# Gated DeltaNet mixing loop: the in-chunk couplings made, masked and turned four heads at a time, the cross-chunk couplings behind them

## The chip, the cores and the metric

The kernel runs on one core of one Trainium2 chip. The metric is the device time of one launch in microseconds. Before the change the median of three runs is 1443.28 us (lowest 1442.0, highest 1451.61).

## What is computed

One inference step of a one-layer decoder trunk: RMSNorm, one input projection, two head groups side by side (sliding-window attention and a gated DeltaNet), an output projection, a mixture of experts, a per-layer embedding and a last norm. There are 1024 prompt tokens and 8 decode tokens, all float32. The part that the change touches is the DeltaNet in its chunked form. For each head and each chunk of 64 tokens the reference makes

```python
A = jnp.where(strict, jnp.einsum('bhncd,bhnjd->bhncj', kb, k) * decay, 0.0)
sol = lax.linalg.triangular_solve(eye + A, rhs, left_side=True, lower=True, unit_diagonal=True)
u, w = sol[..., :dv], sol[..., dv:]
qk = jnp.where(causal, jnp.einsum('bhncd,bhnjd->bhncj', q, k) * decay, 0.0)
...
v_new = u_c - jnp.einsum('bhcd,bhde->bhce', w_c, S)
o = jnp.einsum('bhcd,bhde->bhce', qg_c, S) + jnp.einsum('bhcj,bhje->bhce', qk_c, v_new)
S = S * gl_c[..., None, None] + jnp.einsum('bhcd,bhce->bhde', kd_c, v_new)
```

so each 64x64 matrix `eye + A` (8 heads, 16 chunks) has to be inverted or solved with, before the state `S` can go from one chunk to the next.

## The kernel before

The kernel runs stage by stage, each engine with a program of its own and semaphores between them. The mixing stage walks over 8 tiles of 128 prompt tokens: tile 0 stands by itself (it also carries the decode tokens' output projection), tiles 1 to 7 are a loop. A tile holds two chunks of 64 tokens, one on the lower 64 partitions and one on the upper 64 (`HB[0]` and `HB[1]`), and all eight heads along the free dimension. A group `g` is four heads; `hs` is its slice.

The inverse of `eye + A` is built by doubling. `MT` begins as the unit matrix. Level 0 copies the couplings that its mask allows from `ATd` into `MT`; then each of five levels turns `MT` into `T_` on VectorE, multiplies `ATd` by `T_` on TensorE into PSUM, copies that to `Xs` on ScalarE, multiplies `Xs` by `MT` on TensorE, and copies what the level's mask allows into `MT` on VectorE again. The VectorE half is `fill(t, l)` (masked copy at line 1163, turn at line 1166, both four heads at a time and 128x256). The TensorE half is `level(t, l)`: for both groups the first product, which waits for that group's `T{g}`, then for both groups the second, which waits for that group's `X{g}` (all at line 1431, 16 small matmuls for each group and product, 64 for a level). In level 1 the second products also wait for `S`, the state update of line 1089.

What stands around it, in the order in which each engine's program is written:

- VectorE (`tile`): norms and decays of this tile; the outputs of the tile before (line 1104 ends that, `gated`); the small rows at lines 1200 to 1204; then the couplings. Line 1209 multiplies the Gram matrix `G` (PSUM) by the decays `E_` into `ATd`, all eight heads, once for each chunk (64x512, two instructions); line 1212 waits for both and multiplies `ATd` by `betn` in place (128x512); line 1213 makes `ATo`, the couplings of the second chunk to the first (64x512); line 1214 calls `fill(t, 0)`. Then `state` (line 1089), `gated_out` (lines 1108 to 1113), `largest(t, 1)` (lines 1139 to 1144) and `fill(t, 1)`.
- TensorE (`tile`): the Gram matrices (line 1482), the state increments (1393), twelve output-projection matmuls of the tile before (line 1405, 128x512), `level(t, 1)`, then the query-key products (line 1492), which wait for `ATo` because they write the PSUM banks that it reads, `level(t, 2)`, `turn_out` (1399), `level(t, 3)`, and on.
- ScalarE: the exponentials of `E_`, those of attention group 0, then the two copies of level 1 (line 1322), those of attention group 1 (they wait for `largest(t, 1)`, line 1144), then the copies of level 2.
- GpSimd: the mask of the decays (`Em`, line 1042, 128x1024) and then two powers of 128x8 (line 1025), about when VectorE makes the couplings.

A VectorE instruction that reads what the one before it wrote waits on a semaphore that this one raises; there are such waits before line 1212 (`ATd`) and between the masked copy and the turn (`MT{g}`). No queue of DMAs is issued from the touched lines.

Of the kernel before, what the change touches and what calls it, by code (L numbers as in the profile page):

```python
# [29 lines left out]
ALU = mybir.AluOpType  # L30
# [10 lines left out]
AH, HD, GQA = 8, 64, 4  # L41
# [89 lines left out]
def bc(ap, n):  # L131

    return ap.unsqueeze(2).to_broadcast([ap.shape[0], ap.shape[1], n])


def bm(ap, n):

    return ap.unsqueeze(1).to_broadcast([ap.shape[0], n, ap.shape[1]])
# [7 lines left out]
def program(nc, I, O):  # L146
# [3 lines left out]
    def S(name):  # L150
        if name not in sems:
            sems[name] = nc.alloc_semaphore(name=f"{name}_{len(stages)}")
        return sems[name]
# [14 lines left out]
    def settle(eng):  # L168

        eng.sem_inc(S(f"settled_{eng.engine}".replace(".", "_")), 1)  # L170
# [4 lines left out]
    with es:  # L175
# [55 lines left out]
        def flat(i, n):  # L231
            return psum[:, i:i + n, :].rearrange("p a b -> p (a b)")
# [715 lines left out]
        E_ = mem.take(NH, P)  # L948
        gU = mem.take(NH, P)
        ATd, ATo = mem.take(NH, HD), mem.take(NH, HD)  # L950
# [9 lines left out]
        ss8, m8, r8, egam, kdec, eglS, gam8, rqp, rq2, bet, betn, rk2, kab = (mem.take(NH) for _ in range(13))  # L960
# [4 lines left out]
        HB = (slice(0, HD), slice(HD, P))  # L965
# [22 lines left out]
        def four(i):  # L988
            return heads(bank(i)[:, 0:4 * HD])

        with nc.Block() as block:
# [71 lines left out]
            def _(v):  # L1063
                V = nc.vector
# [84 lines left out]
                    v.wait_ge(S(f"v_den{g}"), t + 1)  # L1149
                    V.reciprocal(rcp[g], den[g]).then_inc(S(f"rcp{g}"), 1)  # L1150

                def fill(t, l):

                    for g in range(2):
                        hs = slice(4 * g, 4 * g + 4)
                        if l == 0:
                            v.wait_ge(S("ATn"), t + 1)
                            v.wait_ge(S("eye"), t + 1)
                        else:
                            v.wait_ge(S(f"PT{g}_ps"), LV * t + l)  # L1160
                        settle(v)
                        mask = cst[:, C_LV + l * P:C_LV + l * P + HD].bitcast(I32)
                        V.copy_predicated(MT[:, hs], bm(mask, 4), ATd[:, hs] if l == 0 else four(6 + g)).then_inc(S(f"MT{g}"), 1)  # L1163
                        if l < LV:
                            v.wait_ge(S(f"MT{g}"), (LV + 1) * t + l + 1)
                            V.transpose(T_[:, hs].rearrange("p h d -> p (h d)"), MT[:, hs].rearrange("p h d -> p (h d)")).then_inc(S(f"T{g}"), 1)  # L1166

                def tile(t, R, dst, first=False):
# [36 lines left out]
                    v.wait_ge(S("E"), t + 1)  # L1205
                    v.wait_ge(S("G_ps"), t + 1)
                    G = flat(4, 2).rearrange("p (h i) -> p h i", i=P)
                    for b in range(2):
                        V.tensor_tensor(ATd[HB[b]], G[HB[b], :, HB[b]], E_[HB[b], :, HB[b]], ALU.mult).then_inc(S("ATd"), 1)
                    v.wait_ge(S("ATd"), 2 * t + 2)  # L1210
                    v.wait_ge(S("v_betn"), t + 1)
                    V.tensor_tensor(ATd, ATd, bc(betn, HD), ALU.mult).then_inc(S("ATn"), 1)
                    V.tensor_tensor(ATo[HB[0]], G[HB[0], :, HB[1]], E_[HB[0], :, HB[1]], ALU.mult).then_inc(S("ATo"), 1)
                    fill(t, 0)
                    if not first:
                        state(t - 1)
                        gated_out(t - 1)
                    largest(t, 1)
                    fill(t, 1)
                    v.wait_ge(S("QK_ps"), t + 1)  # L1220
                    v.wait_ge(S("Em"), t + 1)
                    V.tensor_tensor(QK, flat(4, 2).rearrange("p (h i) -> p h i", i=P), Em, ALU.mult).then_inc(S("QK"), 1)
                    fill(t, 2)
                    v.wait_ge(S("vraw"), t + 1)
                    v.wait_ge(S("v_kab"), t + 1)
# [18 lines left out]
                v.wait_ge(L("wr"), 32)  # L1244
                V.tensor_tensor(wr, wr, bc(g_ffn, NG + NE), ALU.mult).then_inc(S("wr_gain"), 1)
                tile(0, DEC, lg[0:DEC, NT, :], first=True)
                with v.Fori(1, NT) as t:
                    tile(t, P, lg[:, bass.ds(t - 1, 1), :].rearrange("p a n -> p (a n)"))
# [1051 lines left out]
```

## Time and profile before

| | us |
|---|---|
| median of three runs | 1443.28 |
| the three runs | 1442.0, 1443.28, 1451.61 |
| the profiled execution's own time | 1437.78 |
| its span, from first to last instruction | 1436.0 |
| what lies around the span | 1.78 |
| mean granted TensorE clock over the span | 0.947 |
| TensorE busy (matmul) | 1273.1 |
| VectorE busy | 620.6 |
| ScalarE busy | 375.3 |
| GpSimd busy | 208.6 |

The mixing loop takes from about 380 to 800 us of the span. In the views, PE is TensorE, PEld its weight loads, DVE is VectorE, ACT is ScalarE, POOL is GpSimd. "decode_and_mix" is the room in SBUF that all tiles of this stage share, so the groups have to be told apart by line. A row of a timeline gives start (us from the span's start), length, engine, line, operation, shapes, count, and in brackets the idle time before it with what ended it. A row of the windows gives the stretch, its length, and the busy time (and number of instructions) of PE, PEld, DVE, ACT and POOL, then the granted clock (1.00 is full), the DMA share and GB/s.

### The profile page before, as it was taken

The numbers are of one execution on the slowest core, as the hardware profiler recorded it, in microseconds if no ns is written. First come the engines' busy times: TensorE is split into PE (matmuls) and PEld (weight loads), VectorE is DVE, ScalarE is ACT, GpSimd is POOL, SyncE is SP. The second block draws the span as 40 slices with busy tenths as digits, with TensorE's granted clock in tenths as the row PEclk, the third lists the DMA queues.
The fourth block names the chain that finished last, engine by engine and source line by source line (L and its number), as shares of the span: only waits on it lengthen the run. The fifth ranks groups of instructions, "written<-read, shape, count | busy, mean of one in ns | idle before, by whom it ended". The sixth has DMA issues, their size and how long they took to land. (4 is left out here: it accounts for less than half of the span.)

```text
span 1436.0 us, 21846 instructions
## 1 busy us (share of the span) xinstructions
PE 1273.1 (89%) x8380; PEld 876.8 (61%) x8380; DVE 620.6 (43%) x1130; ACT 375.3 (26%) x735; POOL 208.6 (15%) x275
## 2 busy tenths in 40 slices
PE   6999999954698899999898759899999999974997
PEld 4669999942466676676676534444444454434776
DVE  2323555127756756757757134121111112106564
ACT  2322223111234334334434112111111111113332
POOL 0000000002211212212312001122222222110110
PEclk9999999985899999999999779999999999996999
DMA  6211223237320220220220149499999999935451
GB/s 206 90 52 60 88 88 88 76 43 222 94 66 15 78 91 10 81 91 2 89 77 4 44 153 390 151 350 347 339 341 344 352 353 344 345 144 220 150 175 46
DMA packets 151335, 226.08 MB, mean 157 GB/s; under 512 B 12651, under 2 KB 123835, under 8 KB 146670
## 3 DMA queue, kind: packets, MB, share of 16 engines
q1 hardware_dynamic: 130606, 171.27, 36.1%
q10 hardware_dynamic: 11184, 28.48, 5.6%
q0 software_dynamic: 9504, 25.77, 4.6%
q8 instruction: 27, 0.44, 0.1%
q14 instruction: 14, 0.11, 0.0%
HBM read 183.37 MB, written 46.76 MB: 160 GB/s over the span
## 5 line engine op out<-in xcount | busy, mean ns | idle before, releaser
L1657 PE MATMUL psum<-experts 128*128 128x512 f32 x528 | 232.2, 593 | 2.6 <-DVE experts L1679 2.6
L627 PE MATMUL psum<-split_parts 128*128 128x344 f32 x1224 | 194.2, 321 | 0.0
L627 PEld LDWEIGHTS psum<-split_parts 128*128 128x128 f32 x1224 | 193.9, 188 | 0.1
L1657 PEld LDWEIGHTS psum<-experts 128*128 128x128 f32 x528 | 100.5, 191 | 128.0 <-issue 125.0
L1694 DVE COPY experts<-psum 128x256 f32<-128x256 f32 x33 | 14.0, 425 | 274.8 <-PE psum L1664 274.8
L1431 PE MATMUL psum<-decode_and_mix 64*64 64x64 f32 x2560 | 100.8, 228 | 28.7 <-DVE decode_and_mix L1166 21.3
L1431 PEld LDWEIGHTS psum<-decode_and_mix 64*64 64x64 f32 x2560 | 89.2, 140 | 57.3 <-issue 56.8
L1405 PE MATMUL psum<-decode_and_mix 128*128 128x512 f32 x256 | 120.9, 618 | 0.7 <-ACT decode_and_mix L1288 0.7
L1673 PE MATMUL psum<-experts 128*128 128x512 f32 x264 | 119.2, 595 | 1.5 <-ACTq L1710 1.0
L2260 PE MATMUL psum<-last_parts 128*128 128x512 f32 x432 | 103.1, 399 | 0.0
L2260 PEld LDWEIGHTS psum<-last_parts 128*128 128x128 f32 x432 | 82.9, 194 | 17.1
L1025 POOL TENSOR_TENSOR decode_and_mix<-decode_and_mix,lasting 128x8 f32<-128x8 f32 (+2 forms) x33 | 44.0, 1342 | 314.6 <-DVE decode_and_mix L1123 234.9
L1405 PEld LDWEIGHTS psum<-decode_and_mix 128*128 128x128 f32 x256 | 47.7, 196 | 51.3 <-issue 48.8
L1673 PEld LDWEIGHTS psum<-experts 128*128 128x128 f32 x264 | 47.8, 191 | 49.2 <-issue 47.2
L1641 POOL DMA_INDIRECT ye_d<-experts x33 | 33.2, 1006 | 272.0 <-ACT experts L1708 272.0
L1708 ACT ACTIVATE experts<-psum 128x1024 f32<-128x1024 f32 x33 | 33.8, 1023 | 139.0 <-PE psum L1673 139.0
L1701 ACT ACTIVATE experts<-psum 128x256 f32<-128x256 f32 x33 | 12.6, 383 | 196.9 <-PE psum L1657 196.9
L587 PE MATMUL psum<-project 128*128 128x512 f32 x144 | 63.6, 595 | 0.0
L1322 ACT ACTIVATE decode_and_mix<-psum 128x256 f32<-128x256 f32 x80 | 30.5, 381 | 124.0 <-PE psum L1431 121.6
L1679 DVE TENSOR_TENSOR experts<-psum,lasting 128x1024 f32<-128x1024 f32 x33 | 40.4, 1225 | 47.6 <-PE psum L1649 47.6
L1163 DVE COPY_PREDICATED decode_and_mix<-lasting,psum 128x256 f32<-128x256 int32 x80 | 33.6, 430 | 48.6 <-PE psum L1431 48.6
L422 DVE SCALAR_TENSOR_TENSOR project<-project 128x1056 f32<-128x1056 f32 x36 | 47.5, 1319 | 4.7 <-DVE project L418 1.5
(369 smaller groups left out, 1692.0 us busy)
## 6 DMA issues: line engine op xcount, KB each, us to landing
experts<-in_w_gate SPq DMA_DIRECT2D x33, 1024.0 KB, 5.8
experts<-in_w_up SPq DMA_DIRECT2D x33, 1024.0 KB, 10.6
experts<-in_w_down SPq DMA_DIRECT2D x33, 1024.0 KB, 12.3
project<-in_w_in SPq DMA_DIRECT2D x18, 512.0 KB, 4.9
last<-ye_d SPq DMA_DIRECT2D x16, 512.0 KB, 7.1
conv_out_d<-project ACTq DMA_DIRECT2D x12, 512.0 KB, 3.1
decode_and_mix<-conv_out_d SPq DMA_DIRECT2D x8, 768.0 KB, 7.4
until_mixed<-in_x_prompt SPq DMA_DIRECT2D x8, 512.0 KB
```

The costliest lines, as they stand in the source:

```text
L422: nc.vector.scalar_tensor_tensor(yc[:, u, 0:NV], xp[:, u, j:j + NV], cwT[:, ft, j:j + 1], yc[:, u, 0:NV], ALU.mult, ALU.add).then_inc(S(f" ...
L587: mm = nc.tensor.matmul(bank(5 + 2 * u), xT[:, u, k, :], wtok[:, k, 144:], start=(k == 0), stop=(k == KD - 1))
L627: mm = nc.tensor.matmul(thirds(u)[:, b], w[:, u, k, :], x[:, k, b * TB:(b + 1) * TB], start=(i == 0 and k == 0), stop=(i == 2 and k == KD ...
L1025: g.tensor_tensor(out, in_, half[0:out.shape[0]].to_broadcast([out.shape[0], n]), ALU.pow).then_inc(S("r_" + name), 1)
L1163: V.copy_predicated(MT[:, hs], bm(mask, 4), ATd[:, hs] if l == 0 else four(6 + g)).then_inc(S(f"MT{g}"), 1)
L1405: mm = T.matmul(bank(2 + n)[0:R], src[:, k, :], wout[:, k, n * 512:(n + 1) * 512], start=(k == 0), stop=(k == KD - 1))
L1431: mm = T.matmul(bank(out + g)[HB[b], (s % 4) * HD:(s % 4 + 1) * HD], left[HB[b], s, :], right[HB[b], s, :], start=True, stop=True)
L1657: mm = nc.tensor.matmul(bank(2 + s.v), xgT[s.v][:, k, :], wgu[s.u][:, k, :], start=(k == 0), stop=(k == KD - 1))
L1673: mm = nc.tensor.matmul(bank(6 + n), hT[s.v][:, k, :], wd[s.u][:, k, n * 512:(n + 1) * 512], start=(k == 0), stop=(k == KE - 1))
L1679: nc.vector.tensor_tensor(xgT[s.v], flat(0, 2).rearrange("p (k c) -> p k c", c=P), bc(g_ffn, P), ALU.mult).then_inc(S("xgT" + s.h), 1)
L1708: nc.scalar.activation(ye[s.v], flat(6, 2), ACT.Copy).then_inc(S("ye" + s.h), 1)
L2260: mm = nc.tensor.matmul(bank(4 + 2 * (t % 2) + m), x[t % 2][:, k, :], w[:, k, cols], start=(i == 0 and k == 0), stop=(i == 2 and k == KD - 1))
```

## The change

VectorE's program of a tile makes the in-chunk couplings group by group. For four heads it multiplies `G` by `E_` for either chunk (now 64x256 each), waits for the two, multiplies by `betn` (now 128x256), and at once does that group's level 0 of `fill`: masked copy and turn. Then the same for the other four heads. `ATo`, the couplings between the chunks, stood ahead of `fill(t, 0)` and stands behind it now. The semaphores count accordingly: `ATd` rises four times a tile, not two, and `ATn` two times, not one; `fill` at level 0 waits for its own group's count. TensorE, ScalarE, GpSimd and the DMA queues keep their programs.

```diff
-                def fill(t, l):
-
-                    for g in range(2):
+                def fill(t, l, groups=(0, 1)):
+
+                    for g in groups:
                         hs = slice(4 * g, 4 * g + 4)
                         if l == 0:
-                            v.wait_ge(S("ATn"), t + 1)
+                            v.wait_ge(S("ATn"), 2 * t + g + 1)
                             v.wait_ge(S("eye"), t + 1)
...
                     G = flat(4, 2).rearrange("p (h i) -> p h i", i=P)
-                    for b in range(2):
-                        V.tensor_tensor(ATd[HB[b]], G[HB[b], :, HB[b]], E_[HB[b], :, HB[b]], ALU.mult).then_inc(S("ATd"), 1)
-                    v.wait_ge(S("ATd"), 2 * t + 2)
-                    v.wait_ge(S("v_betn"), t + 1)
-                    V.tensor_tensor(ATd, ATd, bc(betn, HD), ALU.mult).then_inc(S("ATn"), 1)
+                    for g in range(2):
+                        hs = slice(4 * g, 4 * g + 4)
+                        for b in range(2):
+                            V.tensor_tensor(ATd[HB[b], hs], G[HB[b], hs, HB[b]], E_[HB[b], hs, HB[b]], ALU.mult).then_inc(S("ATd"), 1)
+                        v.wait_ge(S("ATd"), 4 * t + 2 * g + 2)
+                        v.wait_ge(S("v_betn"), t + 1)
+                        V.tensor_tensor(ATd[:, hs], ATd[:, hs], bc(betn[:, hs], HD), ALU.mult).then_inc(S("ATn"), 1)
+                        fill(t, 0, (g,))
                     V.tensor_tensor(ATo[HB[0]], G[HB[0], :, HB[1]], E_[HB[0], :, HB[1]], ALU.mult).then_inc(S("ATo"), 1)
-                    fill(t, 0)
                     if not first:
                         state(t - 1)
                         gated_out(t - 1)
```

## Rows read from the trace of the kernel before

**Rows 1.** Windows view, one stretch of 50 us inside the mixing loop.

```profile
500.00:550.00 50.00, 47.31 (x558) 34.08 (x554) 32.83 (x74) 18.86 (x42) 11.48 (x8) 1.00 0.21 66
```

**Rows 2.** Waits view, 380 to 800 us: total us, times, longest.

```profile
PE psum L1431 <- DVE decode_and_mix L1166: 21.3, 17, 2.1
```

**Rows 3.** Timeline of PE, tile from 540 us and start of the next.

```profile
539.41 5.42 PE L1405 MATMUL psum<-decode_and_mix 128*128 128x512 f32 x12
546.21 2.73 PE L1431 MATMUL psum<-decode_and_mix 64*64 64x64 f32 x64 [1.38 <-DVE decode_and_mix L1166]
548.87 1.16 PE L1492 MATMUL psum<-decode_and_mix 64*128 64x128 f32 x16
551.35 3.26 PE L1431 MATMUL psum<-decode_and_mix 64*64 64x64 f32 x64 [1.32 <-DVE decode_and_mix L1166]
...
600.75 2.73 PE L1431 MATMUL psum<-decode_and_mix 64*64 64x64 f32 x64 [1.39 <-DVE decode_and_mix L1166]
```

**Rows 4.** Timeline of DVE, the same tile.

```profile
539.68 2.33 DVE L1104 TENSOR_SCALAR decode_and_mix<-decode_and_mix 128x8 f32<-128x8 f32 x1
...
542.39 1.40 DVE L1209 TENSOR_TENSOR decode_and_mix<-psum,decode_and_mix 64x512 f32<-64x512 f32 x2
543.83 0.69 DVE L1212 TENSOR_TENSOR decode_and_mix<-decode_and_mix 128x512 f32<-128x512 f32 x1
544.55 0.68 DVE L1213 TENSOR_TENSOR decode_and_mix<-psum,decode_and_mix 64x512 f32<-64x512 f32 x1
545.16 0.43 DVE L1163 COPY_PREDICATED decode_and_mix<-lasting,decode_and_mix 128x256 f32<-128x256 int32 x1
545.62 0.45 DVE L1166 STREAM_TRANSPOSE decode_and_mix<-decode_and_mix 128x256 f32<-128x256 f32 x1
...
546.79 0.38 DVE L1089 TENSOR_TENSOR decode_and_mix<-decode_and_mix,psum 128x256 f32<-128x256 f32 x1
547.10 0.15 DVE L1108 TENSOR_TENSOR decode_and_mix<-decode_and_mix 128x8 f32<-128x8 f32 x1
...
550.14 0.16 DVE L1144 TENSOR_TENSOR decode_and_mix<-lasting,decode_and_mix 128x4 f32<-128x4 f32 x1
550.28 0.45 DVE L1163 COPY_PREDICATED decode_and_mix<-lasting,psum 128x256 f32<-128x256 int32 x1
...
553.91 0.44 DVE L1163 COPY_PREDICATED decode_and_mix<-lasting,psum 128x256 f32<-128x256 int32 x1 [0.79 <-PE psum L1431]
```

**Rows 5.** Timeline of ACT, the same tile, level 1's first copy.

```profile
546.93 0.38 ACT L1322 ACTIVATE decode_and_mix<-psum 128x256 f32<-128x256 f32 x1 [4.75 <-PE psum L1431]
```

**Rows 6.** Lines by form, DVE, 380 to 800 us: busy, mean ns, idle.

```profile
L1212 DVE TENSOR_TENSOR decode_and_mix<-decode_and_mix 128x512 f32<-128x512 f32 x8 | 5.5, 693 | 0.3
L1239 DVE TENSOR_TENSOR decode_and_mix<-decode_and_mix 128x256 f32<-128x256 f32 x8 | 3.3, 418 | 0.0
```

**Rows 7.** Timelines of PE and DVE, tile 0.

```profile
386.86 2.53 PE L1431 MATMUL psum<-decode_and_mix 64*64 64x64 f32 x64 [2.06 <-DVE decode_and_mix L1166]
390.41 2.40 PE L1431 MATMUL psum<-decode_and_mix 64*64 64x64 f32 x64
388.90 0.45 DVE L1163 COPY_PREDICATED decode_and_mix<-lasting,psum 128x256 f32<-128x256 int32 x1
```

**Rows 8.** Windows view: level 2 of the tile of Rows 3, and of a later tile.

```profile
550.88:555.08 4.20, 3.53 (x67) 3.23 (x68) 3.35 (x7) 2.27 (x10) 0.00 (x0) 0.79 0.00 0
714.47:718.67 4.20, 3.36 (x76) 2.90 (x77) 3.47 (x8) 2.64 (x11) 0.00 (x0) 1.00 0.00 0
```

**Rows 9.** Timeline of PE, level 1 of that later tile and of the next.

```profile
709.83 2.73 PE L1431 MATMUL psum<-decode_and_mix 64*64 64x64 f32 x64 [1.38 <-DVE decode_and_mix L1166]
763.44 2.73 PE L1431 MATMUL psum<-decode_and_mix 64*64 64x64 f32 x64 [1.39 <-DVE decode_and_mix L1166]
```

**Rows 10.** Timeline of POOL, the tile of Rows 3.

```profile
539.63 2.36 POOL L1042 TENSOR_TENSOR decode_and_mix<-decode_and_mix,lasting 128x1024 f32<-128x1024 f32 x1
542.10 3.23 POOL L1025 TENSOR_TENSOR decode_and_mix<-decode_and_mix,lasting 128x8 f32<-128x8 f32 x2
```

## The prediction

> **What bounds the kernel now.** I looked first at the windows view over the mixing loop. In a stretch of 50 us TensorE is busy 47.31 us and VectorE 32.83 [rows 1], so on average TensorE bounds the loop. That is an average; what is left over has to be read from the places where TensorE stands still. The waits view names one place that matters here: the small matmuls of the inverse (L1431) wait for VectorE's turns (L1166), 21.3 us in all, 17 times [rows 2]. That total is the most that this change could ever earn.
>
> The PE timeline shows where in a tile these waits lie. In the tile from 540 us TensorE ends its twelve projection matmuls at 539.41 + 5.42 = 544.83 and stands 1.38 us before level 1 starts at 546.21. Level 1 and the query-key products end at 548.87 + 1.16 = 550.03, and TensorE stands again, 1.32 us, before level 2 at 551.35 [rows 3]. One pair of waits comes in each of the seven looped tiles. The change aims at the first of the pair. Whether it earns anything depends on the second.
>
> So the third view is VectorE's timeline between the two. From 539.68, where L1104 starts, no idle time stands ahead of any VectorE instruction until level 2's masked copy at 553.91, which shows 0.79 us [rows 4]. Between level 0's `fill` and level 1's `fill` stand the state update (546.79), the gated outputs (from 547.10) and the second group's maxima (last one at 550.14). The masked copy of level 1 starts at 550.28, directly behind them. What it reads, the second products of level 1, is nearly done by then: TensorE has gone over to the query-key products at 548.87, so both groups are there 1.4 us before VectorE is. Thus level 2 does not wait for level 1. It waits for VectorE to work through its list. The reader should see two different things in two waits of one name: before level 1, TensorE waits for the couplings; before level 2, it waits for whatever VectorE's list still holds, however early level 1 was done.
>
> **The change, part by part.** It removes nothing and adds three VectorE instructions per tile: four products of 64x256 in place of two of 64x512, two of 128x256 in place of one of 128x512. It moves `ATo` behind level 0.
>
> *The list up to level 1's fill.* Before, from the first coupling (542.39) to the state update (546.79) is 4.40 us [rows 4]. By starts: the two 64x512 products 1.44 (to 543.83), `betn` 0.72 (to 544.55), `ATo` 0.61 (to 545.16), both groups' masked copies and turns 1.63 (to 546.79). The same rows show what a neighbour costs: `betn` lasts 0.69 and the next starts 0.03 after its end, while `ATo` lasts 0.68 and the next starts 0.07 before its end. `betn` follows a wait on its own engine's result; in the new order a wait of that kind also stands behind each `betn`, since the masked copy reads it. So I count length + 0.03 where the next instruction waits for this one, and length - 0.07 where it does not.
>
> The lengths of the halves: the form of the new `betn` is there, 128x256 from SBUF at 418 ns, against 693 ns for the whole 128x512 [rows 6]. For a 64x256 product with one operand in PSUM the nearest rows are that 0.42 and the 0.38 of the 128x256 state update, also with a PSUM operand [rows 4]. I take 0.41, since the whole ones (0.68 to 0.70) are almost as long as `betn`. Per group: first product 0.41 - 0.07 = 0.34, second 0.41 + 0.03 = 0.44, `betn` 0.42 + 0.03 = 0.45, together 1.23. Two groups 2.46, against 1.44 + 0.72 = 2.16 before. The copies, turns and `ATo` keep 1.63 and 0.61. The list grows by 0.30 us. Bounds: with 0.38 for all three forms, 2 x (0.31 + 0.41 + 0.41) - 2.16 = +0.10; with 0.42 for all, 2 x (0.35 + 0.45 + 0.45) - 2.16 = +0.34. A shorter list is excluded, because no work goes away and the rows show that half the elements cost well over half the time. The Trainium skill, VectorE: DVE Perf Modes, section on the TRN2 errata, says that operations from SBUF pay a fixed cost per instruction, about 150 cycles as measured, and advises 512 elements or more; it speaks against the split. At 0.96 GHz (the same page) three extra ones would be an estimated 0.47 us per tile, 3.3 us in seven, where the rows give 0.30 and 2.1.
>
> *The gain ahead of level 1.* The first group's turn now ends about 542.39 + 1.23 + 0.46 + 0.45 = 544.53 (copy to turn 0.46, turn 0.45 long [rows 4]), before TensorE is free at 544.83. The 1.38 us go away, but only for 16 of the 64 matmuls. The second group's turn, which ended about 0.07 behind the state update's start, at 546.86, now ends at about 546.86 - 0.61 + 0.30 = 546.55, so TensorE stops again after about 0.7 us of work. Behind the second group's first product stands the wait for the state update, which the moved `ATo` pushes: it ended at 547.17 and now ends at 547.47. Before, ScalarE's copy of the first group ended at 546.93 + 0.38 = 547.31 [rows 5] and set the second products; now the state update does. So level 1 ends at about the same time as before, 0.1 to 0.2 us earlier. `ATo` itself, needed by the query-key products, is there at 547.2, well before the 548.87 at which they started. That move costs nothing, and if its cover were gone, it would cost its 0.61 us at most.
>
> *Where the stall goes.* Level 1's `fill` starts 0.30 us later, since it is behind VectorE's list; so does the turn that releases level 2, and level 2 starts at 551.65. The stall of 1.38 us is not saved: it is moved behind the first 16 matmuls and then into the wait before level 2. Behind level 2 there is no cover: VectorE waits for TensorE again at 553.91 [rows 4], so 0.30 us per tile goes straight to the end. ScalarE's second exponentials also start behind VectorE's last maximum and shift along.
>
> *Tile 0.* There is no state update and no gated output, and level 2 follows without idle time ahead of it, after 2.06 us ahead of level 1 [rows 7]. Level 1 gains some tenths here, but VectorE's copy at 388.90 also moves by 0.30, which takes them back. I count 0; the bounds are -2.06 and +0.34.
>
> *The clock.* In level 2 of the tile from 540 us the granted clock is 0.79 over the window, in that of a later tile 1.00 [rows 8]: part of the window ran at 1.2 GHz, after the two stops. From level 1 to level 1 the first tile takes 600.75 - 546.21 = 54.54 us and the later one 763.44 - 709.83 = 53.61 [rows 3, 9]: a dip costs 0.93 us. The same two windows laid over all seven looped tiles give four with a dip (0.77 to 0.81) and three at 1.00. The change shifts idle time from before level 1 to before level 2, which could bring a dip to the other three (+2.8 us) or, with other timing, take four away (-3.7 us). I count no change and keep both ends.
>
> *Sum.* 7 x 0.30 = 2.1 us. Against the profiled execution: 1437.78 (span 1436.0 and 1.78 around it) + 2.1 = 1439.9. The median lies 5.5 us above that execution, so on its scale: 1443.28 + 2.1 = **1445.4 us**.
>
> **The rivals.**
>
> *TensorE sets the pace after all.* If VectorE's list had slack that the timeline hides, the 1.38 us would be earned in each looped tile: 7 x 1.38 = 9.7, and 2.06 in tile 0, so 11.7 us: 1443.28 - 11.7 = 1431.6. For it: 21.3 us of waits, and it is the first group's turn that releases level 1. Against it: the unbroken VectorE row and the second wait in the same tile. Even then the gain is 0.8%. Faster by over 1% needs 14.4 us, that is, the second wait must shrink too. I give this 6 in 100 within 1%, and 3 in 100 beyond it together with fewer dips.
>
> *VectorE is held by GpSimd.* L1104, eight elements wide, lasts 2.33 us beside GpSimd's mask product (539.63 to 541.99) and ends with it [rows 4, 10]. Directly behind run GpSimd's two powers, 542.10 to 545.33 [rows 10]. The first group's `betn` and its masked copy now fall inside that stretch (`betn` at 542.39 + 0.34 + 0.44 = 543.17), where the copy used to start at 545.16. If the powers held them as the mask held L1104, `betn` would start at 545.33: 2.16 us per tile, 7 x 2.16 = 15.1 us, so 1445.4 + 15.1 = 1460.5, slower by 1.2%. It decides from 12.3 us on, 1.76 per tile. Against it: before, `betn` itself started at 543.83, within the powers, and lasted the usual 0.69. The Trainium skill, SBUF — State Buffer, section SBUF: two separate sides, says that a VectorE operation in a two-port mode, or with two SBUF inputs, and a GpSimd operation that reads SBUF exclude each other for the whole instruction. L1104 looks like it, and `betn` beside the powers does not. I give it 5 in 100.
>
> *The clock falls in all seven tiles.* 1445.4 + 2.8 = 1448.2, still within 1%. For it: the stop ahead of level 2 grows from 1.32 to about 1.7 us. 20 in 100; dips gone altogether (1441.7), 10 in 100.
>
> **How the numbers follow.** Forecast, VectorE's list sets level 2 and the clock stays as it is: 56. Clock in all seven: 20; in none: 10; TensorE sets the pace: 6, and 3 beyond 1%; GpSimd holds VectorE: 5. About 1% is what a measurement of this kernel can tell from no change, as its three runs are 9.6 us apart. So faster 0.03, same 0.92, slower 0.05. The range takes in the clock's two ends with the list's bounds, 1445.4 - 3.7 - 1.4 = 1440.3 and 1445.4 + 2.8 + 0.3 = 1448.5, and the spread of runs around their median, mostly upward: 1437 to 1452.
>
> **What would show it.** Right, if in the changed trace the idle time ahead of level 1 is near 0, that within level 1 has grown, that ahead of level 2 has grown to 1.5 us or more, and VectorE has no idle time from L1104 to level 1's last turn, with some 4.7 us from the first coupling to the state update. Wrong, if the masked copy of level 1 waits for TensorE (then the gain is real), if a half product or a copy beside GpSimd's powers lasts over 1 us (then it is held), or if the windows of level 2 show a clock other than a mixture of 0.8 and 1.0.

## The result and the profile after

The changed kernel takes 1459.12 us (median of 4 runs, 1454.9 to 1464.11) against 1442.64 us: a ratio of 1.0106 with a 95% interval of 1.0055 to 1.0157. The same kernel timed again beside the experiments gave 1456.6 us (9 runs, 1451.73 to 1459.47) against 1445.94, a ratio of 1.0076 (1.0047 to 1.0105). It is slower by about 1%. The forecast was 1445.4 with a range from 1437 to 1452: the direction of the step was right, its size was not.

The kernel before spreads over 20 us: 85 runs beside the experiments lie between 1435.75 and 1455.58, with a median of 1445.3. Its profiled execution (1437.78) is thus one of its shorter ones. The profiled execution after takes 1456.79 us (span 1455.0, mean granted clock 0.934).

First VectorE's timeline, in the changed kernel, of the tile that answers to [rows 4]:

```profile
553.12 0.87 DVE L1211 TENSOR_TENSOR decode_and_mix<-psum,decode_and_mix 64x256 f32<-64x256 f32 x2
554.02 0.43 DVE L1214 TENSOR_TENSOR decode_and_mix<-decode_and_mix 128x256 f32<-128x256 f32 x1
554.63 0.45 DVE L1163 COPY_PREDICATED decode_and_mix<-lasting,decode_and_mix 128x256 f32<-128x256 int32 x1 [0.18 <-DVE decode_and_mix L1214]
555.11 0.45 DVE L1166 STREAM_TRANSPOSE decode_and_mix<-decode_and_mix 128x256 f32<-128x256 f32 x1
555.59 0.88 DVE L1211 TENSOR_TENSOR decode_and_mix<-psum,decode_and_mix 64x256 f32<-64x256 f32 x2
...
558.06 0.68 DVE L1216 TENSOR_TENSOR decode_and_mix<-psum,decode_and_mix 64x512 f32<-64x512 f32 x1
558.67 0.40 DVE L1089 TENSOR_TENSOR decode_and_mix<-decode_and_mix,psum 128x256 f32<-128x256 f32 x1
...
562.18 0.44 DVE L1163 COPY_PREDICATED decode_and_mix<-lasting,psum 128x256 f32<-128x256 int32 x1
```

From the first coupling to the state update is now 558.67 - 553.12 = 5.55 us, where it was 4.40. The forecast had 4.70. The list is 1.15 us longer, and the rows say by what: a pair of half products takes 0.90 us up to `betn`, so 1.80 for all four where the two whole ones took 1.44; each masked copy of level 0 has an idle time of 0.18 us ahead of it that ends with VectorE's own `betn` product; and behind each turn the next product starts 0.48 us after the turn's start, where it was 0.37 between turn and state update.

Then TensorE's timeline, for the same tile of the changed kernel, the answer to [rows 3]:

```profile
550.13 5.42 PE L1407 MATMUL psum<-decode_and_mix 128*128 128x512 f32 x12
555.70 0.68 PE L1433 MATMUL psum<-decode_and_mix 64*64 64x64 f32 x16
558.17 0.68 PE L1433 MATMUL psum<-decode_and_mix 64*64 64x64 f32 x16 [1.79 <-DVE decode_and_mix L1166]
559.22 1.15 PE L1433 MATMUL psum<-decode_and_mix 64*64 64x64 f32 x32 [0.36 <-DVE decode_and_mix L1089]
560.29 1.16 PE L1494 MATMUL psum<-decode_and_mix 64*128 64x128 f32 x16
563.25 3.64 PE L1433 MATMUL psum<-decode_and_mix 64*64 64x64 f32 x64 [1.79 <-DVE decode_and_mix L1166]
```

Level 1 starts 0.15 us after the projection matmuls (before: 1.38), as the change intends. It then does 16 matmuls and stops for 1.79 us until the second group is turned, stops again for 0.36 until the state update that the moved `ATo` pushed back, and stops for 1.79 ahead of level 2, where it was 1.32. Three stops in place of two, and level 2 starts 563.25 - 553.12 = 10.13 us after the first coupling, where it was 8.96: 1.17 us later, which is the growth of the list.

How long the looped tiles became shows between these two tiles of the changed kernel (first products of level 1). The clock falls to 1.2 GHz for 3.4 us in every looped tile of this execution (such a short fall is called a dip here), but in this one within level 1 and the query-key products, where no time is lost by it, as shown further down:

```profile
611.07 0.68 PE L1433 MATMUL psum<-decode_and_mix 64*64 64x64 f32 x16 [0.15 <-DVE decode_and_mix L1166]
...
665.85 0.68 PE L1433 MATMUL psum<-decode_and_mix 64*64 64x64 f32 x16 [0.15 <-DVE decode_and_mix L1166]
```

54.78 us, against 53.61 for a tile without a dip before [rows 9]: 1.17 us more. In seven looped tiles that is 8.2 us. Where the kernel before has a costly dip, its tile takes 54.54 us [rows 3, 9], and there the changed kernel is only 0.24 us longer: the longer list takes the place of the dip's cost.

Most of the rest is at the end of the loop's first pass. TensorE's timeline there and the window behind it, in the changed kernel:

```profile
469.77 0.64 PE L1420 MATMUL psum<-decode_and_mix 128*128 128x36 f32 x4
471.82 2.57 PE L1420 MATMUL psum<-decode_and_mix 128*128 128x36 f32 x12 [1.41 <-issue]
474.32 1.97 PE L1369 MATMUL psum<-decode_and_mix 64*64 64x64 f32 x16
...
471.50:489.00 17.50, 17.18 (x89) 12.93 (x89) 7.98 (x17) 0.00 (x0) 0.61 (x1) 0.51 0.19 58
```

TensorE waits 1.41 us, in the middle of the routing matmuls, for nothing that these views show, and for 17.5 us from there the granted clock is 0.51, that is 1.2 GHz, while the engine is busy 98% of the time. The 16 small matmuls of line 1369 take 1.97 us in it; a pass later they take 1.14. The first looped tile is 64.2 us long instead of 55.6. Windows of half a microsecond from 380 us to a little behind the loop add up to 30.7 us at 1.2 GHz before and 64.8 after.

The trace's record of transfers tells more of that wait: a 16 KB transfer on a queue named "instruction" runs from 469.32 to 470.46 us, and TensorE goes on 1.36 us after its end. Nine profiles of this study have the wait, and in each TensorE goes on 1.2 to 1.5 us after the end of such a transfer, which began between 466.9 and 473.3 us; in the four without the wait it began between 464.3 and 465.8. So the wait goes with instructions that come late. What makes them late is not shown.

Over the mixing loop, from the first looped tile's couplings to the last state update, the profiled executions differ by 398.53 - 382.50 = 16.0 us: 8.2 of VectorE's list, and 7.8 net of clock and first pass (the first looped tile alone is 8.6 longer, list included). Another 3.0 us lie behind the loop, where VectorE's couplings have no part.

### The profile page after: what moved, and what is told of

Read it like the earlier page. It is cut to its first block and busy times, and to the rows that moved or that the text cites. A ratio compares the mean times of both kernels' runs of the same rounds, so it can differ in the third digit from the quotient of the medians.

```text
span 1455.0 us, 21899 instructions
## 1 busy us (share of the span) xinstructions
PE 1289.3 (89%) x8380; PEld 889.0 (61%) x8380; DVE 626.3 (43%) x1154; ACT 375.4 (26%) x735; POOL 209.0 (14%) x275
```

## The experiments

Each kernel was timed against the kernel before on the same chip; the last section has a single run. The time at 1.2 GHz of a run is worked out as twice (1 - granted clock) times its span, and given as the mean over a kernel's runs. "List" is the time from the first coupling to the state update, and "tile" a looped tile without a dip; in the changed kernel, e3 and e8, which have a dip in every looped tile, it is one whose dip lies in level 1 and the query-key products. One of the twelve runs of e4 took 4698.73 us, which nothing here explains; its median counts that run, its ratio and its time at 1.2 GHz do not.

| kernel | list us | tile us | median us | ratio (95%) | at 1.2 GHz, us |
|---|---|---|---|---|---|
| before (85 runs) | 4.40 | 53.61 | 1445.3 | | 162 |
| changed (second timing) | 5.55 | 54.78 | 1456.6 | 1.0076 (1.0047 to 1.0105) | 187 |
| e1_ato_behind | 4.67 | 53.89 | 1452.84 | 1.0043 (1.0022 to 1.0065) | 179 |
| e2_split_only | 4.84 | 54.05 | 1448.02 | 1.0022 (0.9996 to 1.0047) | 163 |
| e3_pad | 5.30 | 54.54 | 1455.08 | 1.0071 (1.0046 to 1.0095) | 180 |
| e4_after_gated_later | 5.55 | 54.06 | 1454.76 | 1.0060 (1.0037 to 1.0083) | 181 |
| e5_before_gated_later | 4.40 | 52.90 | 1438.33 | 0.9961 (0.9933 to 0.9989) | 154 |
| e7_half_betn_gated_later | 4.48 | 52.99 | 1445.76 | 1.0001 (0.9973 to 1.0028) | 166 |
| e8_after_conv_later | 5.54 | 54.77 | 1452.29 | 1.0071 (1.0042 to 1.0100) | 187 |
| e9_before_conv_later | 4.40 | 53.62 | 1446.64 | 1.0009 (0.9984 to 1.0034) | 163 |
| e10_gated_conv_later | 4.40 | 52.90 | 1437.61 | 0.9949 (0.9929 to 0.9969) | 152 |

### Only the cross-chunk couplings moved

```diff
-                    V.tensor_tensor(ATo[HB[0]], G[HB[0], :, HB[1]], E_[HB[0], :, HB[1]], ALU.mult).then_inc(S("ATo"), 1)
                     fill(t, 0)
+                    V.tensor_tensor(ATo[HB[0]], G[HB[0], :, HB[1]], E_[HB[0], :, HB[1]], ALU.mult).then_inc(S("ATo"), 1)
```

> Nothing is split; only the cross-chunk couplings go behind level 0's fill. Theory A (the changed kernel is slow because VectorE's list before level 1's fill grew, 4.40 to 5.55 us per tile, by waits on its own results that nothing covers): the list here stays at 4.4 us, so the time stays within 2 us of the kernel before, the stop ahead of level 1 falls from 1.38 to about 0.8 us and that ahead of level 2 grows by about as much. Theory B (it is slow because TensorE's stops were moved and with them the stretches at 1.2 GHz grew, 30.7 to 64.8 us in the mixing loop): the stops move here too, so 5 to 15 us slower with more time at half clock.

Measured: the list grows to 4.67 us with the same instructions. VectorE's timeline in this kernel:

```profile
555.27 0.69 DVE L1212 TENSOR_TENSOR decode_and_mix<-decode_and_mix 128x512 f32<-128x512 f32 x1
556.14 0.45 DVE L1163 COPY_PREDICATED decode_and_mix<-lasting,decode_and_mix 128x256 f32<-128x256 int32 x1 [0.18 <-DVE decode_and_mix L1212]
...
557.43 0.45 DVE L1166 STREAM_TRANSPOSE decode_and_mix<-decode_and_mix 128x256 f32<-128x256 f32 x1
557.90 0.68 DVE L1214 TENSOR_TENSOR decode_and_mix<-psum,decode_and_mix 64x512 f32<-64x512 f32 x1
558.51 0.40 DVE L1089 TENSOR_TENSOR decode_and_mix<-decode_and_mix,psum 128x256 f32<-128x256 f32 x1
```

`ATo` had covered the masked copy's wait for `betn`. Without it the copy starts 0.87 us after `betn` started, of which 0.18 is idle, where `ATo` came after 0.72. And the product behind a turn starts 0.47 after the turn, not 0.37. Theory A had said 4.4 us and 2 us at most; the list accounts for 7 x 0.27 = 1.9 of the 8.1 us between this median and that of the kernel before beside it (1444.72). The rest goes with 17 us more at 1.2 GHz, so theory B is nearer here.

Not every wait for VectorE's own result costs 0.18 us. `betn` waits for the product directly ahead of it and starts 0.04 after that one's end (542.39 + 1.40 and 543.83 in [rows 4]), and the turn, which waits for the masked copy, starts 0.03 after its end. The masked copy is the only VectorE instruction of the tile whose program raises a semaphore of its own (`settle`) between the waits and the instruction. Whether that or the form of the instruction makes it dearer was not tested.

### Only the split, with every wait covered

Only the added lines are shown, against the kernel before:

```diff
+                    for g in range(2):
+                        hs = slice(4 * g, 4 * g + 4)
+                        for b in range(2):
+                            V.tensor_tensor(ATd[HB[b], hs], ...).then_inc(S("ATd"), 1)
+                    for g in range(2):
+                        hs = slice(4 * g, 4 * g + 4)
+                        v.wait_ge(S("ATd"), 4 * t + 2 * g + 2)
+                        v.wait_ge(S("v_betn"), t + 1)
+                        V.tensor_tensor(ATd[:, hs], ATd[:, hs], bc(betn[:, hs], HD), ALU.mult).then_inc(S("ATn"), 1)
                     V.tensor_tensor(ATo[HB[0]], ...).then_inc(S("ATo"), 1)
                     fill(t, 0)
```

> All six half instructions as in the change, but all six ahead of the cross-chunk couplings and of both fills, so that each one's wait on VectorE's own result is covered by another. Theory A: the list is 4 x 0.45 + 2 x 0.35 + 0.61 + 1.63 = 4.74 us, 0.34 more than before, 2.4 us in seven tiles; most of the 1.15 us of the changed kernel is then the order, not the number of instructions. Rival A2 (a half instruction costs as much more anywhere): list 5.3 us or more, 6 us or more slower. Theory B: stops stay where they were before, so within 3 us of the kernel before whatever the list does.

Measured: list 4.84 us, 0.44 more than before. VectorE's timeline in this kernel:

```profile
606.66 1.77 DVE L1211 TENSOR_TENSOR decode_and_mix<-psum,decode_and_mix 64x256 f32<-64x256 f32 x4
608.46 0.76 DVE L1216 TENSOR_TENSOR decode_and_mix<-decode_and_mix 128x256 f32<-128x256 f32 x2
609.25 0.68 DVE L1217 TENSOR_TENSOR decode_and_mix<-psum,decode_and_mix 64x512 f32<-64x512 f32 x1
...
611.49 0.38 DVE L1089 TENSOR_TENSOR decode_and_mix<-decode_and_mix,psum 128x256 f32<-128x256 f32 x1
```

The four half products take 1.80 us from start to start of the next line, 0.45 each; the 1.44 for two whole ones was 0.72 each. They do not overlap, though none of them waits for another. The time at 1.2 GHz is that of the kernel before (163 us), and 7 x 0.44 = 3.1 us of list stand against 2.7 us to the median of the 85 runs (3.3 to that of the runs beside it; the ratio's interval takes in 1). So the split costs 0.44 us of the 1.15, and the order the remaining 0.71. Of the latter 0.27 is there without a split (e1); the other 0.44 comes only when the halves are made and filled in turn, since each group then has an uncovered `betn` and a product behind its turn.

### The list longer by a pad

```diff
                     if not first:
+                        V.tensor_tensor(osq, vn, vn, ALU.mult)
+                        V.tensor_tensor(pad[:, 0:4], vn[:, 0:4], vn[:, 0:4], ALU.mult)
                         state(t - 1)
```

> The kernel before with two VectorE instructions that nobody uses (128x512 and 128x256 products) ahead of the state update: the list grows by 0.61 + 0.33 = 0.94 us and nothing else changes. Theory A: level 2 starts 0.94 us later in each of seven tiles, 6.6 us slower. Theory B: the longer stop ahead of level 2 also brings more time at half clock, so 10 to 16 us slower. A third reading (VectorE's list has slack): within 2 us of before.

Measured: list 5.30 us (+0.90), tile 54.54 (+0.93), 7.1 per mille slower. A slack in VectorE's list is excluded: what is put into it comes out of the tile, to within 0.03 us. The list is 6.3 of the 9.8 us to the median of the 85 runs, between what theory A and theory B had said, and the kernel spends 18 us more at 1.2 GHz.

### The gated outputs behind level 1's fill

In the kernel before (e5), and the same edit in the changed kernel (e4):

```diff
                     if not first:
                         state(t - 1)
-                        gated_out(t - 1)
                     largest(t, 1)
                     fill(t, 1)
+                    if not first:
+                        gated_out(t - 1)
```

> The kernel before with the gated outputs moved from ahead of level 1's fill to behind it; couplings as they were (list 4.40 us). Theory A (VectorE's list sets level 2): level 2 starts about 1.3 us earlier in each looped tile, directly behind the query-key products, a looped tile without a clock dip takes about 52.3 us where it took 53.6, and the kernel is about 9 us faster (1436). Theory B (only the time at half clock matters): faster by 0.45 us for each us at half clock that goes away, at least 4 dips of 3.4 us, 6 us. If the turned-out rows then hold TensorE, the same time as before.

> The changed kernel with the gated outputs (three VectorE instructions, 1.5 us) moved from ahead of level 1's fill to behind it. Theory A: the list falls to about 4.0 us plus the maxima, level 2 starts as soon as level 1 and the query-key products are done, and the kernel is 5 to 10 us faster than the kernel before (1433 to 1438). Theory B: stops shrink, so the time at half clock falls too and the gain is larger, 10 us or more. If VectorE's list is not what holds level 2: no change against the changed kernel (1457).

Measured in the kernel before: 0.9961, with no dip of the clock in its looped tiles. TensorE's timeline in that kernel:

```profile
548.88 1.16 PE L1493 MATMUL psum<-decode_and_mix 64*128 64x128 f32 x16
549.97 2.60 PE L1432 MATMUL psum<-decode_and_mix 64*64 64x64 f32 x64
553.19 0.66 PE L1400 MATMUL psum<-lasting,decode_and_mix 128*128 128x128 f32 x4 [0.61 <-DVE decode_and_mix L1223]
554.11 2.73 PE L1432 MATMUL psum<-decode_and_mix 64*64 64x64 f32 x64 [0.27 <-DVE decode_and_mix L1166]
```

Level 2 follows the query-key products at once, 1.38 us earlier than in [rows 3]. That confirms that VectorE's list was what held it. Of the 1.3 us 0.7 are earned (52.90 against 53.61), because the list now holds the next thing in it: TensorE waits 0.61 for VectorE's masked query-key product (L1223) and 0.27 for level 3's turn. In the changed kernel the same edit does the same to a tile without a dip. TensorE's timeline of such a tile in e4:

```profile
561.83 1.16 PE L1495 MATMUL psum<-decode_and_mix 64*128 64x128 f32 x16
563.25 2.74 PE L1434 MATMUL psum<-decode_and_mix 64*64 64x64 f32 x64 [0.26 <-DVE decode_and_mix L1166]
566.61 0.66 PE L1402 MATMUL psum<-lasting,decode_and_mix 128*128 128x128 f32 x4 [0.61 <-DVE decode_and_mix L1225]
```

Level 2 waits 0.26 us in place of 1.79, and from first coupling to first coupling the tile takes 54.06 us, 0.72 less than in the changed kernel. It is also 1.16 more than in e5 (52.90), with no dip in either: the longer list costs the same here too. Yet the median moved from 1456.6 to 1454.8 only, where 7 x 0.72 would be 5 us; the two intervals do not exclude that. Theory A had said 1433 to 1438, so it missed: the edit takes three instructions away from ahead of level 2, but the couplings keep their 1.15 us, which is some 8 us in seven tiles over e5. And its profile has 14 us at 1.2 GHz twice, at the end of the first looped tile and in the second:

```profile
533.00:547.00 14.00, 14.00 (x68) 9.96 (x67) 8.95 (x20) 0.65 (x1) 0.61 (x1) 0.51 0.14 46
```

No such wait stands ahead of the second one, and TensorE has no idle time in it at all.

### A cheaper way to the same early turn

Whole products, only `betn` in two halves back to back, fills, `ATo` behind, and the gated outputs late:

```diff
-                    V.tensor_tensor(ATd, ATd, bc(betn, HD), ALU.mult).then_inc(S("ATn"), 1)
-                    V.tensor_tensor(ATo[HB[0]], ...).then_inc(S("ATo"), 1)
+                    for g in range(2):
+                        hs = slice(4 * g, 4 * g + 4)
+                        V.tensor_tensor(ATd[:, hs], ATd[:, hs], bc(betn[:, hs], HD), ALU.mult).then_inc(S("ATn"), 1)
                     fill(t, 0)
+                    V.tensor_tensor(ATo[HB[0]], ...).then_inc(S("ATo"), 1)
...
```

> Whole 64x512 products, only the product with the write strengths in two halves back to back (each covers the other's wait), then both fills of level 0, then the cross-chunk couplings, and the gated outputs behind level 1's fill. Theory A: first turn 0.6 us earlier than before, list about 4.5 us, and with the gated outputs out of it the kernel is 10 to 13 us faster than before (1432 to 1435). Theory B: no stop over 1 us is left ahead of level 1 or 2, so few dips, 10 us or more faster. If the order itself is harmful (cross-chunk couplings late): slower than the same kernel with only the gated outputs moved.

Measured: 1.0001, where theory A had said 1432 to 1435 us. List 4.48 and tile 52.99, both 0.08 to 0.09 above e5: an earlier first turn earns nothing, and the list's growth comes out again in full. 1445.76 against 1438.33 of e5 is more than the list gives (0.6 us); its profile has the wait in the first pass and 13.6 us at 1.2 GHz behind it, which e5's has not.

### Is it the burst of transfers?

The load of the next tile's convolved rows (768 KB) runs just when TensorE waits in the first pass: in the changed kernel it is issued at 463.96 us and lands 8.7 us later. Three kernels issue it later: the changed one (e8), the one before (e9) and e5 (e10).

```diff
                     sp.wait_ge(S("kS_ps"), t)
+                    sp.wait_ge(S("av_ps"), t)
                     settle(sp)
                     load_conv(sp, rows)
-                    sp.wait_ge(S("av_ps"), t)
                     settle(sp)
                     load_values(sp, t)
```

> The changed kernel, with the 768 KB load of the next tile's convolved rows issued about 18 us later (behind the attention's last products, together with the values), so that no burst of transfers runs while TensorE's program of the loop's first pass comes in. Theory F (TensorE's 1.4 us wait for its own instructions at the routing matmuls, and the 14 to 17 us at half clock behind it, come from that burst): both are gone, 6 to 8 us faster than the changed kernel, 1449 to 1451, which is the kernel before plus VectorE's longer list (7 x 1.17 = 8.2 us) less what dips it hides. If the wait stays: 1457 or above, and the burst is not its cause. Later loads may cost up to 1 us per tile at the turn of the rows, 7 us, in either case.

> The control: the kernel before with the same later load. Theory F: its two profiles had no long stretch at half clock at that place, so nothing is won, within 2 us of the kernel before; plus up to 7 us if the later load is waited for at the turn of the rows, which its timeline would show as a stop ahead of that line.

> The fastest version so far (the kernel before with the gated outputs behind level 1's fill, 1438) with the later load. Theory F: its profile too had no long stretch there, so nothing is won in the loop, 1436 to 1440. If slow runs of that kernel come from the burst, the spread of its runs shrinks from 20 us to 10 or less.

Measured in e8, the first pass of TensorE's timeline and the window behind it:

```profile
470.73 0.64 PE L1420 MATMUL psum<-decode_and_mix 128*128 128x36 f32 x4
471.98 1.79 PE L1420 MATMUL psum<-decode_and_mix 128*128 128x36 f32 x12 [0.61 <-issue]
...
472.50:486.50 14.00, 14.00 (x78) 10.42 (x77) 7.18 (x13) 0.00 (x0) 0.61 (x1) 0.51 0.39 121
```

and in e9:

```profile
472.83 1.42 PE L1418 MATMUL psum<-decode_and_mix 128*128 128x36 f32 x12 [0.88 <-issue]
...
473.00:487.00 14.00, 13.99 (x122) 10.72 (x123) 11.27 (x27) 3.08 (x8) 0.77 (x2) 1.00 0.39 122
```

In e8 the load is issued at 471.04 us, 7 us later and not the 18 of the expectation, and other loads still move up to 412 GB/s until shortly ahead of the wait; so the burst is less, not gone. The wait is 0.61 us in place of 1.41, and the long stretch at 1.2 GHz stays. In e9 the wait is 0.88, and the clock stays at 1.00 through the same matmuls. Over the profiles, the wait is 0.61 and 0.88 us where the load was moved and 1.41 to 2.23 in the seven others that have it, and the kernel before has none with the load in its old place. So theory F falls for the clock: neither this load nor the wait decides alone whether it falls. For the wait, the load may lengthen it; it does not make it. e8's median, 1452.29, lies between the two forecasts and 4 us below the changed kernel's, within the two intervals. e9 changes nothing. e10 has the lowest median, 0.9949 (0.9929 to 0.9969) of the kernel before, but is not clear of e5 (1438.33); its runs spread over 13.9 us, those of e5 over 19.8, where 10 or less was expected if the burst made the longer ones.

### The kernel before, once more

> The kernel before once more, for a second profile. If the wait for instructions near the end of the loop's first pass and the long stretch at half clock belong to the changed order alone, they are absent again. If they are chance, they may be here, and the run is then nearer 1448 than 1438 us.

1436.62 us, with three single dips, no wait at the routing matmuls and no long stretch. In the profiles at hand the wait there is absent in before (twice), e5 and e10, and present in the changed kernel (twice), e1, e2, e3, e4, e7, e8 and e9; all of these but e9 have the long stretch behind it. For the changed kernel, the second profile showed the same wait (1.43) and 13.7 us at 1.2 GHz, and all nine runs of that timing lie above 1450 us. Both profiles of the kernel before are of short executions, 1437.78 and 1436.62 us where the median is 1445.3, so they do not show whether its usual execution has the long stretch too; that of e9, at 1447.51, has not.

## Why the prediction was wrong, and where it was right

**What bounds the tile: right.** VectorE's list sets level 2. The list grew by 0.27, 0.44, 0.90 and 1.15 us in e1, e2, e3 and the changed kernel, and the tile by 0.28, 0.44, 0.93 and 1.17; in e1 and e2 that is a tile without a dip.

**Where the stall goes: right.** It moved behind the first 16 matmuls, as said. The stop ahead of level 1 went from 1.38 to 0.15, and the one ahead of level 2 grew to 1.79 where no dip fills it (predicted: about 1.7). Level 1 was to end 0.1 to 0.2 us earlier, which failed: the query-key products behind it start 560.29 - 553.12 = 7.17 us after the first coupling, where it was 6.48. This cost nothing by itself, as VectorE's list ended later still.

**The sum of the list: wrong, by a factor of nearly four.** +0.30 was forecast, with +0.34 as the upper bound; +1.15 was measured. The lengths were good (0.42 to 0.44 for the halves, against 0.41 and 0.42). The spacings failed. Per group: the pair of products takes 0.90, not 0.34 + 0.44 = 0.78, since products on the lower and the upper partitions do not overlap; the 1.40 for two in [rows 4], twice the 0.68 to 0.69 of one, had said so. The copy comes 0.61 after `betn`, not 0.45, since 0.18 idle stands before it. The turn is followed after 0.48, not 0.37, and comes 0.48 after the copy, not 0.46. That makes 2.47 per group in place of 2.06, and 0.8 us for both. I took the price of a wait from `betn` to `ATo`, but `ATo` does not wait for `betn`: no row of before shows the masked copy directly behind the product that it reads. An operation that had stood as a cover was costed as moved for nothing ("That move costs nothing"), and e1 shows what its cover was worth: 0.27 us per tile, 0.15 of it ahead of the copy.

**Tile 0: wrong, it was counted as nothing.** The bounds were -2.06 and +0.34. From its first coupling to that of the next tile, tile 0 takes 50.36 us in the five profiles with the old couplings and no dip there (before twice, e3, e9, e10), and 51.34 in e4, which has the changed couplings and no dip there either: 0.98 us, for a list 1.1 us longer. In the two profiles of the changed kernel, with a dip, it takes 51.91 and 52.09. By the lists as measured, the sum would have been 7 x 1.17 + 0.98 = 9.2 us, 1452.5 on the scale of the prediction's 1443.28, at the upper end of its range.

**The rule of fixed cost per instruction.** The Trainium skill, VectorE: DVE Perf Modes, section on the TRN2 errata, would have given an estimated 0.47 us per tile for three more instructions. The trace agrees for the split alone (e2: 0.44 us); the 0.71 that come from the order are not in that rule.

**Clock: the end of the range was too near.** I counted single dips at 0.93 us and at most three more. In the changed kernel's profile there is a dip in tile 0 and in each of the seven looped tiles. Those that fall into level 1 and the query-key products cost nothing, as VectorE's list is the slower there: this stretch of the changed kernel,

```profile
669.36 1.87 PE L1433 MATMUL psum<-decode_and_mix 64*64 64x64 f32 x32 [0.36 <-DVE decode_and_mix L1089]
671.16 1.99 PE L1494 MATMUL psum<-decode_and_mix 64*128 64x128 f32 x16
673.40 2.74 PE L1433 MATMUL psum<-decode_and_mix 64*64 64x64 f32 x64 [0.24 <-DVE decode_and_mix L1166]
```

runs largely at half clock, the stop ahead of level 2 shrinks to 0.24, and the tile still takes 54.8 us, as much as a tile without a dip (53.61) and the longer list (1.15) make together. What had no place in the forecast was a long stretch: 17.5 us in one tile, about 7.5 us lost (64.2 us, less 54.8 and about 2 that the first pass cost before too). Between the medians (1445.3 and 1456.8 over both timings) lie 11.5 us; the list is 9.2 of them, tile 0 included, if tiles without a costly dip are compared, as shown by the tile lengths. That the other 2.3 are clock is argued only, from the 187 to 195 us at 1.2 GHz against 162; and since the longer list hides dips that cost time before, the two parts are not independent.

**The rivals.** GpSimd holding VectorE would have given 1460.5, near the first median, but for the wrong reason: beside GpSimd's powers, which run from 552.82 to 556.05 in the tile shown,

```profile
552.82 3.23 POOL L1025 TENSOR_TENSOR decode_and_mix<-decode_and_mix,lasting 128x8 f32<-128x8 f32 x2
```

the new `betn` lasts 0.43 and nothing lasts over 0.88 for two. TensorE setting the pace is excluded by e3. The clock in all seven tiles came true in the profiles of the changed kernel and was cheap; the long stretch was the dear part.

**What stays open.** Why the clock falls for 14 to 17 us in the first passes of some kernels, with TensorE busy throughout, and stays at full in others behind a wait of the same kind (e8 against e9). It went with the changed order in both of its profiles, but also with e1's and e3's, whose products are not split, and e4 shows such a stretch with no wait ahead of it. Whether the usual execution of the kernel before has one is not known. A kernel that differs from the changed one in that stretch alone was not found.

## What to carry to other kernels

Before splitting an instruction so that its consumer can start earlier, ask whether that consumer's engine is waiting for this result or for the end of the other engine's whole list; in the second case every added start and every uncovered wait comes out of the tile one to one, and shortening the list (here: three instructions moved behind the next release point, 0.7 us per tile) earns what an earlier first result does not. The price of a wait on an engine's own result must be read where producer and consumer stand next to each other; an unrelated instruction between them is a cover, and moving it away has a price. And where TensorE's stops are moved, keep a long stretch at the lower clock in the range, not only single dips.

## What the runs showed of the hardware

- VectorE: a masked copy directly behind the product that it reads starts 0.18 us after the product's end; with an unrelated product in between no such idle time appears. A product that waits for the one directly ahead of it starts 0.03 to 0.04 after its end, so the price of a wait is not one number. Products of 64x256 on the lower and upper 64 partitions follow each other every 0.45 us, halves of 128x256 back to back every 0.38 to 0.40 (0.76 for two).
- TensorE's clock: in the profiles of the changed kernel 17 and 13.7 us at 1.2 GHz with the engine busy 98% and more, though in the looped tiles of the kernel before stops of 1.4 us had been followed by 3.4 us at most. A dip of 3.4 us that begins in level 2 costs 0.93 us in the kernel before; one in level 1 and the query-key products of the changed kernel costs nothing. Within the 85 runs of the kernel before, a run with 1 us more at 1.2 GHz is about 0.4 us longer (slopes of 0.39 to 0.43 in three sets of runs); the runs have 138 to 183 us at 1.2 GHz, which goes with most of their 20 us of spread.
- Instructions: in the loop's first pass TensorE stood still for 0.6 to 2.2 us in nine profiles, and went on 1.2 to 1.5 us after the end of a 16 KB transfer on the instruction queue.
- GpSimd: VectorE's eight-element L1104 again lasts 2.33 us beside GpSimd's mask product, while products of 128x256 beside its powers take their usual time.
